# Software-pipelining two row loops of a hybrid attention and MLP block on eight cores

## What is computed

```python
def _rms_norm(x, w):
    xf = x.astype(jnp.float32)
    y = xf * lax.rsqrt(jnp.mean(xf * xf, axis=-1, keepdims=True) + EPS)
    return (y * w.astype(jnp.float32)).astype(x.dtype)

u = _rms_norm(h, norm1_w[layer])            # h is x: (32, 2048, 1024) float32
proj = u @ w_in[layer]                      # 1024 -> 2840 columns
...                                         # two groups of 8 heads: sparse attention, stick-breaking attention
mixed = jnp.concatenate([_head_rms_norm(o_nsa, ...), _head_rms_norm(o_sb, ...)], axis=-1)
h = h + mixed @ w_out[layer]                # 1024 -> 1024, residual
u = _rms_norm(h, norm2_w[layer])
up = u @ w_up[layer]                        # 1024 -> 5632
up = conv_general_dilated(up, ...)          # depthwise, width 3, causal
gate, val = up[..., :D_FF], up[..., D_FF:]
h = h + (jax.nn.silu(gate) * val) @ w_down[layer]
return _rms_norm(h, final_norm_w)
```

## Time and profile before

| | us |
|---|---|
| timed executions | 10073.04 and 10159.66, median 10116.35 |
| profiled execution, its own time | 10038.94 |
| its span on the slowest core (core 5) | 10037.4 |
| spans of the eight cores | 10002.9 to 10037.4 |
| TensorE matmuls busy | 6969.3 (69%) |
| VectorE busy | 5220.1 (52%) |
| ScalarE busy | 4658.9 (46%) |
| GpSimd busy | 718.5 (7%) |

### The profile page before, as it was taken

One profiled execution on the slowest core, in us unless ns is written; L12 is line 12 of the kernel. 1 busy time (PEld: TensorE's weight loads), 2 busy tenths in 40 slices (PEclk: granted clock), 3 DMA queues, 4 the chain that ended last, 5 costly groups with the idle time before them and its releaser, 6 DMA issues.

```text
span 10037.4 us, 162765 instructions; the slowest of 8 cores (10002.9 to 10037.4 us)
## 1 busy us (share of the span) xinstructions
PE 6969.3 (69%) x45344; PEld 3278.1 (33%) x45344; DVE 5220.1 (52%) x14130; ACT 4658.9 (46%) x9893; POOL 718.5 (7%) x850
## 2 busy tenths in 40 slices
PE   0667878577676787756757678766776677785677
PEld 0334433223233343222324344322323444332232
DVE  8244377365525447727632535753672443674555
ACT  0226589332215658823321575862232265794322
POOL 0000000022100000003200000000230000000222
PEclk9857855579977775569977786557997678555899
DMA  0200000244320000033421000013332000001342
GB/s 14 59 7 1 14 1 2 61 76 86 73 46 1 1 14 2 1 86 64 88 78 27 1 2 14 1 28 86 72 66 77 16 1 11 5 2 53 78 87 60
DMA packets 144525, 367.33 MB, mean 37 GB/s; under 512 B 14336, under 2 KB 14976, under 8 KB 143136
## 3 DMA queue, kind: packets, MB, share of 16 engines
q0 software_dynamic: 96128, 186.01, 11.4%
q1 hardware_dynamic: 47520, 170.90, 5.0%
HBM read 475.74 MB, written 67.11 MB: 54 GB/s over the span
## 4 chain that ended last, share of the span: by engine, by line
PE 40%; DVE 29%; issue 13%; ACT 8%; DMA 7%; DVEq 2%; ACTq 0%; SPq 0%; POOL 0%; POOLq 0%
PE ps L356 37%; DVE arena L381 15%; DVE arena L372 10%; ACT arena L369 6%; DMA arena<-w_up_r 3%; PE ps L359 3%; DMA arena<-out 3%; DVEq L133 2%; DVE arena L387 1%; ACT arena L385 1%; DVE arena L376 1%; DMA arena<-w_out_r 1%; DVE arena L404 1%; DMA arena<-w1r 1%; ACT L369 1%
## 5 line engine op out<-in xcount | busy, mean ns | idle before, releaser
L356 PE MATMUL ps<-arena 128*128 128x512 bf16 (+7 forms) x43168 | 6731.6, 302 | 1725.2 <-DVE arena L372 451.0
L356 PEld LDWEIGHTS ps<-arena 128*128 128x128 bf16 (+1 forms) x43168 | 3104.5, 105 | 5326.0 <-issue 3810.5
L369 ACT ACTIVATE arena<-arena 128x4 f32<-128x4 f32 (+8 forms) x3264 | 1355.2, 445 | 2671.2 <-DVE arena L372 1554.6
L372 DVE TENSOR_TENSOR arena<-arena 128x256 f32<-128x256 f32 (+12 forms) x3745 | 1511.4, 407 | 438.8 <-ACT arena L369 129.3
L369 ACT ACTIVATE arena<-ps 128x512 bf16<-128x512 f32 (+3 forms) x2736 | 1331.3, 534 | 716.0 <-PE ps L356 574.6
L369 ACT ACTIVATE arena<-ps,arena 128x512 bf16<-128x512 f32 (+4 forms) x2688 | 1295.4, 547 | 666.5 <-PE ps L356 638.7
L372 DVE TENSOR_TENSOR arena<-ps,arena 128x256 f32<-128x256 f32 (+5 forms) x2064 | 874.7, 424 | 1365.9 <-PE ps L356 856.8
L359 PE MATMUL ps<-arena 128*128 128x128 bf16 (+2 forms) x2176 | 382.9, 308 | 1326.1 <-DVE arena L381 895.1
L381 DVE SCALAR_TENSOR_TENSOR arena<-ps,arena 128x511 f32<-128x511 f32 (+1 forms) x1408 | 1055.4, 750 | 219.4 <-ACT arena L961 129.3
L381 DVE SCALAR_TENSOR_TENSOR arena<-arena 128x1 f32<-128x1 f32 (+4 forms) x1848 | 741.1, 401 | 205.7 <-DVE arena L392 17.1
L376 DVE TENSOR_SCALAR arena<-ps 128x4 f32<-128x4 f32 (+1 forms) x560 | 183.8, 328 | 1180.2 <-PE ps L356 1180.0
(11 more groups left out here) (27 smaller groups left out, 642.5 us busy)
## 6 DMA issues: line engine op xcount, KB each, us to landing
arena<-w_up_r POOLq DMA_DIRECT2D x352, 256.0 KB, 4.8
arena<-x SPq DMA_DIRECT2D x128, 512.0 KB, 4.3
out<-arena SPq DMA_DIRECT2D x128, 512.0 KB, 2.9
arena<-w_down_r POOLq DMA_DIRECT2D x8, 5632.0 KB, 40.0
arena<-out SPq DMA_DIRECT2D x64, 512.0 KB, 4.4
arena<-w_in_r POOLq DMA_DIRECT2D x116, 256.0 KB, 4.3
arena<-w1r POOLq DMA_DIRECT2D x4, 2048.0 KB, 14.3
arena<-w_out_r POOLq DMA_DIRECT2D x4, 2048.0 KB, 15.6
```

Source lines behind the costliest of these rows:

```text
L356: S.op('pe', lambda e, o=out, l=lhsT, rr=rhs, s0=start, s1=stop, sk=skip: e.matmul(o, lhsT=l, rhs=rr, start=s0, stop=s1, skip_group_check= ...
L369: S.op('act', lambda e, o=out, i=in_, f=func, k=kw: e.activation(out=o, in_=i, func=f, **k), r=r, w=w)
L372: S.op(eng, lambda e, o=out, a=in0, b=in1, p=op: e.tensor_tensor(out=o, in0=a, in1=b, op=p), r=r, w=w)
```

## The change

The norm loop's rows are cut into three stages, called with lags 0, 1, 2: load to scaling; transposes; copy. The output projection's rows are cut into five, with lags 0 to 4: transposes of `mixed`; copy to `mT`; load of x, matmuls, adds, store, and all up to the scaling; transposes of the scaled row; copy to `u2T`. `mT` and `hbuf` become two buffers each, used in turn, with a transfer slot (semaphore) for each store buffer. `ss` and `rstd` get a key for each column, and `junk`, which nothing reads, gets none.

```diff
--- before.py
+++ after.py
@@ -512,19 +512,30 @@
         uT = A.alloc([8, 2048], BF16)
         qkv_m = A.mark()
 
-        memset('dve', ss, 0.0, ['ss'])
+        memset('dve', ss, 0.0, [('ss', i_) for i_ in range(16)])
+        items = []
         for i in range(16):
-            xb = xbuf[i % 2]
-            ub = ubuf[i % 2]
-            S.dma('sp', xb, x_d[b, 128 * i:128 * i + 128, :], slot='x%d' % (i % 2), w=[('xbuf', i % 2)])
-            act(junk, xb, AF.Square, [('xbuf', i % 2)], ['junk', 'ss'], accum=ss[:, i:i + 1])
-            cp('dve', rstd[:, i:i + 1], ss[:, i:i + 1], ['ss'], ['rstd'])
-            rsq(rstd[:, i:i + 1], 1.0 / D, 'rstd')
-            stt('dve', ub, xb, rstd[:, i:i + 1], normw1, ALU.mult, ALU.mult, [('xbuf', i % 2), 'rstd', 'normw1'], [('ub', i % 2)])
-            bk = i % 2
-            for dc in range(8):
-                tp(psb(bk)[:, dc * 128:(dc + 1) * 128], ub[:, dc * 128:(dc + 1) * 128], ident, [('ub', i % 2), 'ident'], [('ps', bk)])
-            cp('act', uT[:, :, 128 * i:128 * i + 128], psb(bk).rearrange("p (a b) -> p a b", a=8), [('ps', bk)], ['uT'])
+            def mk(i=i):
+                xb = xbuf[i % 2]
+                ub = ubuf[i % 2]
+                bk = i % 2
+
+                def sa():
+                    S.dma('sp', xb, x_d[b, 128 * i:128 * i + 128, :], slot='x%d' % (i % 2), w=[('xbuf', i % 2)])
+                    act(junk, xb, AF.Square, [('xbuf', i % 2)], [('ss', i)], accum=ss[:, i:i + 1])
+                    cp('dve', rstd[:, i:i + 1], ss[:, i:i + 1], [('ss', i)], [('rstd', i)])
+                    rsq(rstd[:, i:i + 1], 1.0 / D, ('rstd', i))
+                    stt('dve', ub, xb, rstd[:, i:i + 1], normw1, ALU.mult, ALU.mult, [('xbuf', i % 2), ('rstd', i), 'normw1'], [('ub', i % 2)])
+
+                def sb_():
+                    for dc in range(8):
+                        tp(psb(bk)[:, dc * 128:(dc + 1) * 128], ub[:, dc * 128:(dc + 1) * 128], ident, [('ub', i % 2), 'ident'], [('ps', bk)])
+
+                def sc_():
+                    cp('act', uT[:, :, 128 * i:128 * i + 128], psb(bk).rearrange("p (a b) -> p a b", a=8), [('ps', bk)], ['uT'])
+                return [sa, sb_, sc_]
+            items.append(mk())
+        run_pipeline(items, [0, 1, 2])
 
         def proj_F(dst_fn, scale, keyw):
             wch, wk = w_get()
@@ -901,32 +912,51 @@
         u2T = A.alloc([8, 2048], BF16)
         m_c1 = A.mark()
         wout = A.alloc([8, 1024], BF16)
-        mT = A.alloc([8, 128], BF16)
-        hbuf = A.alloc([1024], F32)
+        mT2 = [A.alloc([8, 128], BF16) for _ in range(2)]
+        hbuf2 = [A.alloc([1024], F32) for _ in range(2)]
         S.dma('pool', wout, wout_d.rearrange("c p n -> p c n"), slot='wout', w=['wout'])
-        memset('dve', ss, 0.0, ['ss'])
+        memset('dve', ss, 0.0, [('ss', i_) for i_ in range(16)])
+        items = []
         for i in range(16):
-            xb = xbuf[i % 2]
-            ub = ubuf[i % 2]
-            S.dma('sp', xb, x_d[b, 128 * i:128 * i + 128, :], slot='x%d' % (i % 2), w=[('xbuf', i % 2)])
-            bk = i % 2
-            for dc in range(8):
-                tp(psb(bk)[:, dc * 128:(dc + 1) * 128], mixed[:, i, dc * 128:(dc + 1) * 128], ident, ['mixed', 'ident'], [('ps', bk)])
-            cp('act', mT, psb(bk).rearrange("p (a b) -> p a b", a=8), [('ps', bk)], ['mT'])
-            for half in range(2):
-                pb = 2 + half
-                for c in range(8):
-                    mm(psf(pb), mT[:, c, :], wout[:, c, 512 * half:512 * half + 512], c == 0, c == 7, ['mT', 'wout'], [('ps', pb)])
-                tt('dve', hbuf[:, 512 * half:512 * half + 512], psf(pb), xb[:, 512 * half:512 * half + 512], ALU.add, [('ps', pb), ('xbuf', i % 2)], ['hbuf'])
-            S.dma('sp', out_d[b, 128 * i:128 * i + 128, :], hbuf, slot='hst', r=['hbuf'], w=[('outh', i)])
-            act(junk, hbuf, AF.Square, ['hbuf'], ['junk', 'ss'], accum=ss[:, i:i + 1])
-            cp('dve', rstd[:, i:i + 1], ss[:, i:i + 1], ['ss'], ['rstd'])
-            rsq(rstd[:, i:i + 1], 1.0 / D, 'rstd')
-            stt('dve', ub, hbuf, rstd[:, i:i + 1], normw2, ALU.mult, ALU.mult, ['hbuf', 'rstd', 'normw2'], [('ub', i % 2)])
-            bk2 = 4 + i % 2
-            for dc in range(8):
-                tp(psb(bk2)[:, dc * 128:(dc + 1) * 128], ub[:, dc * 128:(dc + 1) * 128], ident, [('ub', i % 2), 'ident'], [('ps', bk2)])
-            cp('act', u2T[:, :, 128 * i:128 * i + 128], psb(bk2).rearrange("p (a b) -> p a b", a=8), [('ps', bk2)], ['u2T'])
+            def mk(i=i):
+                xb = xbuf[i % 2]
+                ub = ubuf[i % 2]
+                mT = mT2[i % 2]
+                hbuf = hbuf2[i % 2]
+                bk = i % 2
+                bk2 = 4 + i % 2
+                kh = ('hbuf', i % 2)
+                km = ('mT', i % 2)
+
+                def sa():
+                    for dc in range(8):
+                        tp(psb(bk)[:, dc * 128:(dc + 1) * 128], mixed[:, i, dc * 128:(dc + 1) * 128], ident, ['mixed', 'ident'], [('ps', bk)])
+
+                def sb_():
+                    cp('act', mT, psb(bk).rearrange("p (a b) -> p a b", a=8), [('ps', bk)], [km])
+
+                def sc_():
+                    S.dma('sp', xb, x_d[b, 128 * i:128 * i + 128, :], slot='x%d' % (i % 2), w=[('xbuf', i % 2)])
+                    for half in range(2):
+                        pb = 2 + half
+                        for c in range(8):
+                            mm(psf(pb), mT[:, c, :], wout[:, c, 512 * half:512 * half + 512], c == 0, c == 7, [km, 'wout'], [('ps', pb)])
+                        tt('dve', hbuf[:, 512 * half:512 * half + 512], psf(pb), xb[:, 512 * half:512 * half + 512], ALU.add, [('ps', pb), ('xbuf', i % 2)], [kh])
+                    S.dma('sp', out_d[b, 128 * i:128 * i + 128, :], hbuf, slot='hst%d' % (i % 2), r=[kh], w=[('outh', i)])
+                    act(junk, hbuf, AF.Square, [kh], [('ss', i)], accum=ss[:, i:i + 1])
+                    cp('dve', rstd[:, i:i + 1], ss[:, i:i + 1], [('ss', i)], [('rstd', i)])
+                    rsq(rstd[:, i:i + 1], 1.0 / D, ('rstd', i))
+                    stt('dve', ub, hbuf, rstd[:, i:i + 1], normw2, ALU.mult, ALU.mult, [kh, ('rstd', i), 'normw2'], [('ub', i % 2)])
+
+                def sd_():
+                    for dc in range(8):
+                        tp(psb(bk2)[:, dc * 128:(dc + 1) * 128], ub[:, dc * 128:(dc + 1) * 128], ident, [('ub', i % 2), 'ident'], [('ps', bk2)])
+
+                def se_():
+                    cp('act', u2T[:, :, 128 * i:128 * i + 128], psb(bk2).rearrange("p (a b) -> p a b", a=8), [('ps', bk2)], ['u2T'])
+                return [sa, sb_, sc_, sd_, se_]
+            items.append(mk())
+        run_pipeline(items, [0, 1, 2, 3, 4])
         S.barrier()
         A.release(m_seq)
         actT_lo = A.alloc([16, 1024], BF16)
```

## The result

The changed kernel takes **9540.8 us** in the median of 11 executions (9465.7 to 9630.6), the kernel before 10089.9 (10 executions). The ratio is **0.943, 95% interval 0.939 to 0.948**. The forecast was 9524 with a range of 9430 to 9700.

What follows compares the result with a forecast made beforehand. The prediction took a relay between engines, none full, to bound both loops. Gains of 119 us (norm loop) and 435 (output projection), 554 together, took 10038.9 to 9485, plus 39 for the median: 9524, range 9430 to 9700.

Steps and rivals of the forecast that it cites:

- The relay: In both loops engines wait for each other in turn, none full: 13.65 us per projection row, 5.71 per norm row.
- Norm loop, 119 us: Each of four norm loops falls from 91.3 to 61.6 us, a gain of 29.7 each, 119 in all.
- The ring of the x buffers: Norm loop: two x buffers, each reloaded after its row's scaling, become the new bound at 3.8 us per row.
- The turn: Norm loop: one x buffer's cycle, 3.43 + 0.1 + 4.06 = 7.59 us, serving two rows.
- Rival 3: Both loops: x loads land in 6 to 8 us when rows come faster; 9681 to 9857 us, chance 0.05.
- Output projection, 435 us: Four projection stages, 15 rows each, go from 13.65 to 6.4 us per row: gain 108.8 each, 435 in all.
- The ring: Output projection: second add, store, next x load, landing, first add; 1.20 + 4.3 + 0.05 + 0.86 = 6.4 us per row.
- rival 1: Output projection: TensorE's clock stays at 1.2 GHz or drops each row, 8.7 or 7.9 us per row; 9662 us, chance 0.14.
- VectorE's chain: Output projection: second add, Square, scaling, 4.34 us, and next first add, 0.86; VectorE turns in 5.2 us per row.
- Two hbuf cost nothing: Output projection: doubled hbuf costs nothing and frees the first add from the previous row's scaling; no size given.
- Rival 2: Denser cores push the clock below 2.4 GHz elsewhere, in projections and down-projections, costing 178 us; 9702 us, chance 0.05.
- The sum: Both loops: 119 + 435 = 554 us off 10038.9 gives 9485; 39 added for the median gives 9524.

Runs made afterwards that it cites:

- norm_only: Changed kernel with only the norm loop pipelined, the output projection as in the kernel before; 9902 us on an undisturbed die.
- proj_only: Changed kernel with only the output projection pipelined, the norm loop as in the kernel before; 9582 us on an undisturbed die, ratio 0.965.
- three_x: Changed kernel with three x buffers in the norm loop instead of two; 9415 us on an undisturbed die, ratio 0.939.
- early3: Changed kernel with three x buffers in the output projection and its x load moved to the first stage; 9372 us on an undisturbed die, ratio 0.935.
- six_stages: Changed kernel with three x buffers and early load in both loops, the projection's Square, root and scaling a separate stage; 9286 us on an undisturbed die, 0.927.
- one_hbuf: Changed kernel with a single hbuf and a single store slot; 9472 us on an undisturbed die, ratio 0.948.
- the repeat: The changed kernel run once more unaltered, beside the other experiments on one chip; 9466 us on an undisturbed die, ratio 0.946.
- one_x: Changed kernel with a single x buffer in the norm loop instead of two; 9674 us on an undisturbed die, ratio 0.962.

## Why the prediction was right

*What bounds the kernel.* The relay was the bound in both loops: each loop alone gave about what its stage had lost (112 us in the stage and 119 on the die, 430 and 439), and together they gave the whole, 558.

*Norm loop, 119 us.* Measured 119 by the die (norm_only), 125 by the stages of the changed kernel. The ring of the x buffers was the new limit, as the counts one, two and three buffers show: 446, 239, 184 us. The turn was about 6.9 us and not 7.59, because a load landed in 3.3 us and not in 4.0: 57.4 us in place of 61.6 in the loop shown. The landing is the one term that was mis-sized, and why it fell isn't shown. It isn't that the loads come denser. proj_only has the old norm loop, with a load every 5.7 us, and norm_only the pipelined one, and they landed the other way round (second sequence, core 0, proj_only first):

```profile
DMA to landing us min/median/max: 3.1/3.2/4.5
...
DMA to landing us min/median/max: 3.6/3.8/4.9
```

The quicker landings came with the new output projection, in a loop that it doesn't touch. Rival 3, that denser loads land later, is borne out in kind and not in size: a median of 4.4 us with three buffers (three_x, the loop shown), far from its 6 to 8.

*Output projection, 435 us.* Measured 439 by the die, 432 by its stages. The ring was 6.17 us in the row shown and 6.42 on average over all sequences and cores (6.2 to 6.7 by stage), against 6.4. That the average meets the forecast so closely is partly luck. Over all these loads the landing was 4.05 us in the median and, with single late ones, 4.22 on average, below the 4.3 of the sum; with 4.22 the sum gives 6.33. The remaining 0.1 us fits the rows at the low clock (see rival 1), but was not separated from them. early3 shows that it was this ring: with the load taken out of it, the row fell to 4.97 on average. I had named VectorE's chain as next, and it was, at 4.97 instead of 5.2; TensorE was next after that (six_stages).

*Two hbuf cost nothing and are worth nothing here:* one_hbuf took the same time. 

*Rival 1, TensorE's clock stays low:* ruled out as it was stated, for the whole stage or for each row. But the forecast's clock near 1.00 after the first row held for most rows only. On core 6, the 16 matmuls of a row took over 5 us instead of 3.6 in 8 of the 60 rows behind the first ones of the four sequences (1, 1, 4 and 2), as in the row at 1866.26. The first adds of 56 of these 60 rows were still released by x. In early3, with shorter rows, no row behind the first took that long on any core. Where the Trainium skill's "TensorE: Matmul & The Clock Gate", Part 4: PE-mode transpose, says that transposes don't count toward TensorE being busy as matmuls do, 16 transposes per 16 matmuls didn't keep the clock down in the other 52 rows.

*Rival 2, a lower clock elsewhere:* it happens, but the change isn't shown to cause it. Of the kernel before, 10 of 46 dies (23 executions beside the experiments) had a mean clock more than 0.02 below that kernel's best; of the changed one, 12 of 36 (18 executions). The median execution stands 69 us above the undisturbed die in the kernel before and 89 in the changed one in the series of the result, 122 and 178 in the first series of experiments. So a cost of some tens of us by this rival isn't shown, and isn't excluded either. In the execution shown for the repeat, the same MLP had a mean of 0.84 on one die and 0.94 on the other. The level agrees with the 13/16 that the Trainium skill states in the same page, Part 1: The HAM clock gate. That dense work on three cores of a die brings it on doesn't agree as a rule: in the same execution all eight cores ran the first sequence's projections at 1.00, with TensorE busy in 99.6 to 100 of 100 us. One core of each die (1 and 5):

```profile
340.00:440.00 100.00, 100.00 (x717) 53.96 (x716) 22.41 (x33) 15.39 (x26) 7.91 (x15) 1.00 0.25 38
...
340.00:440.00 100.00, 100.00 (x611) 51.11 (x610) 21.54 (x32) 15.53 (x26) 7.39 (x14) 1.00 0.27 40
```

What sets it off stays open. The median, 9541, stands 75 us above the best executions, more than the 39 that I had added to the sum.

*The sum.* 554 forecast; 555 to 569 on undisturbed dies, 549 between the medians.

## What to carry to other kernels

A loop in which one engine waits for another, row after row, while neither is full is a relay; taking it apart gives up to the longest of the rings that are left, and that is what to compute: for each buffer, from its last reader through the queue and the load to its next reader, divided by the number of buffers. A pipelined loop with too few buffers is slower than a plain one with enough (446 against 364 us). When a load is moved ahead in program order, count the rows in flight: its buffer must have been left by a reader that is called before it, or the load stays in the ring and takes the data of a row not yet read.

## What the runs showed of the hardware

- Loads of 512 KB in the norm loop landed in 3.3 us in the changed kernel, in proj_only and in one_x (3.2 to 3.9 in the median of a loop), and in 3.8 to 3.9 in the kernel before and norm_only (3.6 to 4.2). The difference goes with the version of the output projection and not with how dense the loads come; its cause stays open. With three buffers, two or more in flight, it was 4.4. Behind a store it was 3.9 against 4.3 (first sequence).
- A granted 0.81 comes and goes by die, in kernels before and after alike; a sequence's MLP takes 695 us with about half of it at 0.81 and 674 without, and the two changed stages, bound by a load, take the same. In one_hbuf, cores 2 and 3 had 51 and 57 of their 64 rows at 0.81 (16 matmuls in 4.36 us) and took 502 and 501 us for the projection, cores 0 and 1 had none and took 500 and 503.
- Small loads issued behind one of 5.6 MB on the same queue landed up to 29 us after their issue, and at most 6.5 us after it once that load was cut into 22 (core 4).
